# Norm gains multiplied into the weights during their split, and turned features copied two tiles at a time

## The chip, the cores and the metric

The kernel runs on one core of a Trainium2 chip. The metric is the device time of one execution in microseconds (us). A core has a matrix engine (TensorE, here PE, with its weight loads as PEld), a vector engine (VectorE, here DVE), a scalar engine (ScalarE, here ACT), GpSimd (POOL) and a queue engine (SyncE, SP) that issues the DMA transfers. Each engine runs its own instructions in order and waits on semaphores for the others. SBUF is the on-chip memory of 128 partitions, PSUM holds the results of the matrix engine in 8 banks of 512 float32 per partition.

## What is computed

Four transformer layers on 256 tokens of width 1024, in float32. Each begins its two or three parts with a norm that has a gain vector `g` of one number for each of the 1024 features, and the normed tokens go straight into a matrix product:

```
def rms_norm(x, g):
    xf = x.astype(jnp.float32)
    y = xf * lax.rsqrt(jnp.mean(xf * xf, axis=-1, keepdims=True) + EPS)
    return (y * g.astype(jnp.float32)).astype(x.dtype)

for l in range(DEPTH):                       # first block
    h = rms_norm(x, attn_norm_g[l])
    proj = h @ w_in[l]                       # attention branches, pooling, gates
    ...
    x = x + merged @ w_out[l]
    hf = rms_norm(x, ffn_norm_g[l])
    u = depthwise_conv(hf @ ffn_w_up[l], ffn_conv_w[l], ffn_conv_b[l])
    ...
    x = x + (jax.nn.silu(u_gate) * u_val) @ ffn_w_down[l]
```

A second block of two layers follows: a mixer (stick-breaking attention, then dilated attention), a feed-forward part and a gated embedding, each of which starts with such a norm (`g_mix_pre_2`, `g_ffn_pre_2`, `g_ple_2`).

## The kernel before

**Products from halves.** Every float32 operand is held as two fp32r tiles, `high` (the value rounded to fp32r) and `low` (what is left), and each product is the sum of three matrix passes: high by high, high by low, low by high. So both the weights and the features are split, each by one instruction on ACT (high) and one on DVE (low).

**Weights.** They come from HBM in 476 units of at most 1024 columns: a unit is `nk` row tiles (128 rows of the weight matrix, on the partitions) of `w` columns next to each other. With w = 512 or 416 a unit has two row tiles, with w = 256 four. A unit is loaded by SP into one of 4 buffers `w_raw`, copied by ACT into one of 6 buffers `w_high` (L1444, step "split"), and DVE writes `w_raw - w_high` into `w_low` (L1890). ACT may overwrite a `w_high` only when PE is done with the unit six before it. `Plan.prefetch` puts the split of unit n+5 ahead of the matrix work of unit n, so ACT and DVE run five units ahead of PE where nothing else holds them. PE waits for `w_low` of its unit.

**Features.** Where a norm stands, PE turns (transposes) the tokens by 128x128 blocks into a PSUM bank. ACT copies them out as `x_high`, multiplied by the gain of each feature, which lies on the partition then, and DVE writes `bank * gain - x_high` into `x_low`. The norm's `1/rms` per token is applied elsewhere (to the tokens before the turn, or to the product). Two forms exist. Step `turn` (stages 0, 2, 4 and 7; ACT L1452, DVE L1899) handles all 256 tokens of two feature tiles; there are four for a stage. Step `turn_t` (stages 1, 3, 5, 6, 8 and 9; ACT L1463, DVE L1928) handles 128 tokens of two feature tiles; there are eight for a stage, in two groups of four, one group for each half of the tokens. In both forms ACT and DVE issue one instruction for each feature tile, since each has its own gain column. The next turn into a bank waits for the `x_low` of the one before, and so does the first product that reads it.

**Order.** `Plan` writes one list of steps, and every engine goes through it and issues what is its own. Around a norm the list interleaves turns, sums of squares (ACT L1472 and L1481, DVE L1909) and the splits of the coming units. Stages 0, 2, 4, 5 and 8 also need a `row`: DVE writes two diagonal tiles from `1/rms` (L1958, `squares`), and PE multiplies them by ones (L1149). It stands four units into the new part, or after the tokens of stage 5 or 8.

## Time and profile before

| | us |
|---|---|
| median of 3 runs | 1540.28 |
| lowest, highest | 1540.03, 1543.84 |
| the profiled execution | 1539.27 |
| its span from first to last instruction | 1537.5 |
| PE busy | 1493.6 (97%) |
| DVE busy | 1045.8 (68%) |
| ACT busy | 841.4 (55%) |
| DVE on `w_low` (476 splits) | 570.3 |
| ACT on `w_high` (476 splits) | 495.0 |

The granted clock of PE was 0.999 of full over the span. The profile gives for each engine its busy time, for each group of equal instructions their count and mean, and for each idle time of an engine the instruction that ended it. A timeline row has the start, the time from the start of the first to the end of the last instruction of the row, and in brackets the idle time ahead of it and its releaser. Instructions of one engine overlap a little, so the start of the next instruction tells what one costs in a row.

### The profile page before, as it was taken

The numbers are of one execution on the slowest core, as the hardware profiler recorded it, in microseconds if no ns is written. First come the engines' busy times: TensorE is split into PE (matmuls) and PEld (weight loads), VectorE is DVE, ScalarE is ACT, GpSimd is POOL, SyncE is SP. The second block draws the span as 40 slices with busy tenths as digits, with TensorE's granted clock in tenths as the row PEclk, the third lists the DMA queues.
The fourth block names the chain that finished last, engine by engine and source line by source line (L and its number), as shares of the span: only waits on it lengthen the run. The fifth ranks groups of instructions, "written<-read, shape, count | busy, mean of one in ns | idle before, by whom it ended". The sixth has DMA issues, their size and how long they took to land.

```text
span 1537.5 us, 23829 instructions
## 1 busy us (share of the span) xinstructions
PE 1493.6 (97%) x9824; PEld 1340.0 (87%) x9824; DVE 1045.8 (68%) x1545; ACT 841.4 (55%) x1237; POOL 59.1 (4%) x70
## 2 busy tenths in 40 slices
PE   6999999999999999999999999999999998999998
PEld 5998988998899989799989977998888886799886
DVE  5798677786578877687855567665467557766446
ACT  5465556565456565665643476454456446555434
POOL 1110000000021000000000001000010000100001
PEclk9999999999999999999999999999999999999999
DMA  7543355556555435555566533655656550455661
GB/s 243 161 151 119 129 169 167 186 179 205 182 167 173 130 96 165 173 170 195 173 197 212 167 96 110 208 183 192 193 161 224 181 188 29 160 176 179 205 192 69
DMA packets 72572, 255.73 MB, mean 166 GB/s; under 512 B 8336, under 2 KB 9360, under 8 KB 72464
## 3 DMA queue, kind: packets, MB, share of 16 engines
q1 hardware_dynamic: 72176, 253.78, 51.0%
q8 instruction: 77, 1.26, 0.3%
q10 hardware_dynamic: 288, 0.43, 0.1%
q14 instruction: 31, 0.25, 0.1%
HBM read 253.14 MB, written 1.05 MB: 165 GB/s over the span
## 4 chain that ended last, share of the span: by engine, by line
PE 91%; DVE 5%; ACT 2%; issue 1%; POOL 0%; DVEq 0%; ACTq 0%; POOLq 0%
PE psum L1060 14%; PE psum L1063 14%; PE psum L1062 14%; PE psum L1069 13%; PE psum L1073 13%; PE psum L1071 13%; PE psum L1018 3%; DVE w_low L1890 2%; PE psum L1212 1%; PE psum L1297 1%; PE psum L1242 1%; ACT w_high L1444 1%; DVE dil_weights L2337 1%; DVE x_low L1928 0%; PE psum L1371 0%
## 5 line engine op out<-in xcount | busy, mean ns | idle before, releaser
L1890 DVE TENSOR_TENSOR w_low<-w_raw,w_high 128x1024 fp32r<-128x1024 f32 (+1 forms) x476 | 570.3, 1212 | 267.8 <-ACT w_high L1444 266.3
L1444 ACT ACTIVATE w_high<-w_raw 128x1024 fp32r<-128x1024 f32 (+1 forms) x476 | 495.0, 1050 | 334.4 <-PE psum L1073 188.1
L1060 PE MATMUL psum<-x_high,w_high 128*128 128x256 f32 x1504 | 429.9, 286 | 0.0
L1062 PE MATMUL psum<-x_low,w_high 128*128 128x256 f32 x1504 | 425.5, 283 | 0.0
L1063 PE MATMUL psum<-x_high,w_low 128*128 128x256 f32 x1504 | 425.4, 283 | 0.0
L1060 PEld LDWEIGHTS psum<-x_high,w_high 128*128 128x128 f32 x1504 | 288.4, 192 | 5.3 <-issue 4.6
L1062 PEld LDWEIGHTS psum<-x_low,w_high 128*128 128x128 f32 x1504 | 288.5, 192 | 0.3
L1063 PEld LDWEIGHTS psum<-x_high,w_low 128*128 128x128 f32 x1504 | 288.4, 192 | 0.0
L1069 PE MATMUL psum<-w_high,ff_high 128*128 128x512 f32 x256 | 100.0, 391 | 0.0
L1071 PE MATMUL psum<-w_low,ff_high 128*128 128x512 f32 x256 | 99.6, 389 | 0.0
L1073 PE MATMUL psum<-w_high,ff_low 128*128 128x512 f32 x256 | 99.6, 389 | 0.0
L1069 PE MATMUL psum<-w_high,x_high 128*128 128x512 f32 (+2 forms) x208 | 79.5, 382 | 5.7 <-DVE w_low L1890 4.7
L1073 PE MATMUL psum<-w_high,x_low 128*128 128x512 f32 (+2 forms) x208 | 77.3, 372 | 0.0
L1071 PE MATMUL psum<-w_low,x_high 128*128 128x512 f32 (+2 forms) x208 | 77.2, 371 | 0.0
L1069 PE MATMUL psum<-w_high,x_high_next 128*128 128x512 f32 x192 | 75.7, 394 | 0.0
L1071 PE MATMUL psum<-w_low,x_high_next 128*128 128x512 f32 x192 | 74.8, 390 | 0.0
L1073 PE MATMUL psum<-w_high,x_low_next 128*128 128x512 f32 x192 | 74.8, 389 | 0.0
L1069 PE MATMUL psum<-w_high,ffn_high 128*128 128x512 f32 x176 | 68.7, 390 | 0.0
L1071 PE MATMUL psum<-w_low,ffn_high 128*128 128x512 f32 x176 | 68.5, 389 | 0.0
L1073 PE MATMUL psum<-w_high,ffn_low 128*128 128x512 f32 x176 | 68.5, 389 | 0.0
L1060 PE MATMUL psum<-x_high_next,w_high 128*128 128x256 f32 x224 | 63.5, 284 | 0.0
L1063 PE MATMUL psum<-x_high_next,w_low 128*128 128x256 f32 x224 | 63.4, 283 | 0.0
(264 smaller groups left out, 2389.5 us busy)
## 6 DMA issues: line engine op xcount, KB each, us to landing
w_raw<-in_weights SPq DMA_DIRECT2D x462, 512.0 KB, 4.1
w_raw<-in_weights SPq DMA_DIRECT2D x8, 416.0 KB, 5.7
rows<-in_second_rows SPq DMA_DIRECT2D x4, 512.0 KB, 4.8
w_raw<-in_weights SPq DMA_DIRECT2D x6, 256.0 KB, 2.6
residual<-in_x SPq DMA_DIRECT2D x2, 512.0 KB, 5.9
out<-residual SPq DMA_DIRECT2D x2, 512.0 KB, 2.7
dil_masks<-in_consts SPq DMA_DIRECT2D x1, 576.0 KB, 5.6
rows<-in_pool_w SPq DMA_DIRECT2D x2, 256.0 KB, 5.9
```

What stands on the lines that cost most here:

```text
L1018: return eng.transpose(out, src, ident)
L1060: eng.matmul(o, wh[:, j, cut], high[:, k, :], start=k == 0 and f % 2 == 0, stop=False, skip_group_check=True)
L1062: eng.matmul(o, wh[:, j, cut], low[:, k, :], start=False, stop=False, skip_group_check=True)
L1063: d = eng.matmul(o, wl[:, j, cut], high[:, k, :], start=False, stop=end, skip_group_check=True)
L1069: eng.matmul(o, high[:, k, cut], wh[:, j, :], start=k == 0, stop=False, skip_group_check=True)
L1071: eng.matmul(o, high[:, k, cut], wl[:, j, :], start=False, stop=False, skip_group_check=True)
L1073: d = eng.matmul(o, low[:, k, cut], wh[:, j, :], start=False, stop=end, skip_group_check=True)
L1212: d = eng.matmul(bank[4 + i][:, t * SEQ:(t + 1) * SEQ], qt[i][:, t * P:(t + 1) * P], kt[i], start=True, stop=True)
L1242: d = eng.matmul(bank[6][HD * i:HD * i + HD, 0:SEQ], val, m["probt"][i][:, kt * SEQ:(kt + 1) * SEQ], start=kt == 0, stop=kt == TT - 1, ski ...
L1297: d = eng.matmul(o, m, r, start=False, stop=True, skip_group_check=True)
L1444: act(self.unit_view(self.wh, u), raw, ACT.Copy).then_inc(sem("w_high"), 1)
L1890: tt(self.unit_view(self.wl, u), raw, self.unit_view(self.wh, u), ALU.subtract).then_inc(sem("w_low"), 1)
```

## The change

A unit whose rows are the features of a norm now takes the gain in its split: `high = round(w_raw * gain)` and `low = w_raw * gain - high`. The gain is a number for each row, and a row tile has its own gain column, so the split is one instruction for each row tile. Units of other products are split as before. 304 of the 476 units have a norm ahead of them: 284 of 2 x 512 columns, 8 of 2 x 416 and 12 of 4 x 256. The turned features are then copied without a gain, two feature tiles at a time: `turn` and `turn_t` issue one instruction on ACT and one on DVE, 64 steps in all.

```
+    def unit_gain(self, u):
+        g = {"proj": STAGE_MIX, "gates_early": STAGE_MIX, "gates": STAGE_MIX, "ffn_up": STAGE_FFN,
+             "sb_in": (STAGE_SB,), "sb_values": (STAGE_SB,), "dil_in": (STAGE_DIL,), "dil_qk": (STAGE_DIL,),
+             "dil_values": (STAGE_DIL,), "ff_in": STAGE_FF, "ple_gate": STAGE_PLE}.get(u["name"])
+        return None if g is None else self.gain(g[u["layer"]])[:, u["k0"]:u["k0"] + u["nk"]]
 # ACT
-                act(self.unit_view(self.wh, u), raw, ACT.Copy).then_inc(sem("w_high"), 1)
+                gain, high = self.unit_gain(u), self.unit_view(self.wh, u)
+                if gain is None:
+                    act(high, raw, ACT.Copy).then_inc(sem("w_high"), 1)
+                else:
+                    if not (u["name"] in ("proj", "gates_early", "gates", "ffn_up") and u["layer"] == 0):
+                        q.wait_ge(sem("cols_loaded"), 32)
+                    for j in range(u["nk"]):
+                        c = slice(j * u["w"], (j + 1) * u["w"])
+                        d = act(high[:, c], raw[:, c], ACT.Copy, scale=gain[:, j:j + 1])
+                    d.then_inc(sem("w_high"), 1)
 ...
-                for i in range(2):
-                    k = 2 * part + i
-                    d = act(self.features[g][0][:, k, t * P:(t + 1) * P], bank[b][:, i * P:(i + 1) * P], ACT.Copy,
-                            scale=gain[:, k:k + 1])
-                d.then_inc(sem("tokens_high"), 1)
+                act(self.features[g][0][:, 2 * part:2 * part + 2, t * P:(t + 1) * P], got, ACT.Copy
+                    ).then_inc(sem("tokens_high"), 1)
 # DVE
-                tt(self.unit_view(self.wl, u), raw, self.unit_view(self.wh, u), ALU.subtract
-                   ).then_inc(sem("w_low"), 1)
+                gain, high, low = self.unit_gain(u), self.unit_view(self.wh, u), self.unit_view(self.wl, u)
+                if gain is None:
+                    tt(low, raw, high, ALU.subtract).then_inc(sem("w_low"), 1)
+                else:
+                    for j in range(u["nk"]):
+                        c = slice(j * u["w"], (j + 1) * u["w"])
+                        d = stt(low[:, c], raw[:, c], gain[:, j:j + 1], high[:, c], ALU.mult, ALU.subtract)
+                    d.then_inc(sem("w_low"), 1)
 ...
-                for i in range(2):
-                    k = 2 * part + i
-                    d = stt(low[:, k, c], bank[b][:, i * P:(i + 1) * P], gain[:, k:k + 1], high[:, k, c], ALU.mult,
-                            ALU.subtract)
-                d.then_inc(sem("tokens_low"), 1)
+                tt(low, got, high, ALU.subtract).then_inc(sem("tokens_low"), 1)
```

Step `turn` changes in the same way (`x_high` and `x_low` of 512 columns, one instruction each). The program of PE, POOL and SP is the same instruction for instruction. On ACT and DVE the steps stand in the same order, and only the number of instructions in a step changes. Two places matter.

At the first norm DVE writes the `w_low` of three units ahead of the diagonal tiles of `row`; the same stands at stage 2. Before:

```order
L1899 SCALAR_TENSOR_TENSOR x_low<-psum,cols,x_high 128x256 x4
L1909 ISA squares,stat<-residual 128x512
L1909 ISA stat 128x1
L1918 SCALAR_TENSOR_TENSOR stat<-stat 128x2
L1890 TENSOR_TENSOR w_low<-w_raw,w_high 128x1024 x3
L1958 TENSOR_SCALAR squares<-consts,stat 128x128 x2
```

Now:

```order
L1911 TENSOR_TENSOR x_low<-psum,x_high 128x512 x2
L1919 ISA squares,stat<-residual 128x512
L1919 ISA stat 128x1
L1928 SCALAR_TENSOR_TENSOR stat<-stat 128x2
L1904 SCALAR_TENSOR_TENSOR w_low<-w_raw,cols,w_high 128x512 x4
L1904 SCALAR_TENSOR_TENSOR w_low<-w_raw,cols,w_high 128x256 x4
L1963 TENSOR_SCALAR squares<-consts,stat 128x128 x2
```

Three instructions on `w_low` became eight, the last four those of a unit of 256 columns, and four on `x_low` became two.

At stage 1, between the output product and the feed-forward part, DVE writes two units ahead of the first half's `x_low`. Before:

```order
L1938 TENSOR_TENSOR residual<-residual,psum 128x512 x2
L1945 SCALAR_TENSOR_TENSOR stat<-stat 128x1
L1951 TENSOR_SCALAR scratch<-residual,stat 128x512
L1890 TENSOR_TENSOR w_low<-w_raw,w_high 128x1024 x2
L1928 SCALAR_TENSOR_TENSOR x_low<-psum,cols,x_high 128x128 x4
L1890 TENSOR_TENSOR w_low<-w_raw,w_high 128x1024
L1928 SCALAR_TENSOR_TENSOR x_low<-psum,cols,x_high 128x128 x4
L1938 TENSOR_TENSOR residual<-residual,psum 128x512 x2
```

Now:

```order
L1943 TENSOR_TENSOR residual<-residual,psum 128x512 x2
L1950 SCALAR_TENSOR_TENSOR stat<-stat 128x1
L1956 TENSOR_SCALAR scratch<-residual,stat 128x512
L1904 SCALAR_TENSOR_TENSOR w_low<-w_raw,cols,w_high 128x512 x4
L1935 TENSOR_TENSOR x_low<-psum,x_high 128x2x128 x2
L1904 SCALAR_TENSOR_TENSOR w_low<-w_raw,cols,w_high 128x512 x2
L1935 TENSOR_TENSOR x_low<-psum,x_high 128x2x128 x2
L1943 TENSOR_TENSOR residual<-residual,psum 128x512 x2
```

Each `w_low` became two instructions, and each four of `x_low` two.

## Rows read from the trace of the kernel before

**Rows 1.** The page, busy time of each engine (share of the span, instructions).

```profile
PE 1493.6 (97%) x9824; PEld 1340.0 (87%) x9824; DVE 1045.8 (68%) x1545; ACT 841.4 (55%) x1237; POOL 59.1 (4%) x70
```

**Rows 2.** Waits of PE: for whom, us in total, times, longest.

```profile
PE psum L1149 <- DVE squares L1958: 4.4, 4, 1.6
PE psum L1018 <- DVE x_low L1928: 4.2, 5, 1.2
```

**Rows 3.** Groups by shape: busy us, mean ns of one, idle before them.

```profile
L1890 DVE TENSOR_TENSOR w_low<-w_raw,w_high 128x1024 fp32r<-128x1024 f32 x462 | 558.3, 1222 | 261.4 <-ACT w_high L1444 259.8
L2262 DVE SCALAR_TENSOR_TENSOR residual<-scratch,stat,residual 128x512 f32<-128x512 f32 x16 | 11.3, 749 | 0.9
L1851 DVE SCALAR_TENSOR_TENSOR sb_out_low<-psum,sb_out_high 128x256 fp32r<-128x256 f32 x8 | 3.4, 424 | 13.8 <-ACT sb_out_high L1429 13.8
...
L1444 ACT ACTIVATE w_high<-w_raw 128x1024 fp32r<-128x1024 f32 x462 | 484.3, 1058 | 314.6 <-PE psum L1073 180.9 <-PE psum L1063 121.2 <-DMA w_raw<-in_weights 11.7
L1487 ACT ACTIVATE scratch<-residual,stat 128x512 f32<-128x512 f32 x4 | 2.9, 724 | 3.5 <-POOL stat L2445 3.5
```

**Rows 4.** Timeline of DVE in stage 5: start, us, instruction.

```profile
951.86 1.41 DVE L2262 SCALAR_TENSOR_TENSOR residual<-scratch,stat,residual 128x512 f32<-128x512 f32 x2
953.19 1.22 DVE L1890 TENSOR_TENSOR w_low<-w_raw,w_high 128x1024 fp32r<-128x1024 f32 x1
```

**Rows 5.** Timeline of ACT, DVE and PE at stage 2, up to its row.

```profile
424.69 1.66 DVE L1899 SCALAR_TENSOR_TENSOR x_low<-psum,cols,x_high 128x256 fp32r<-128x256 f32 x4 [1.13 <-ACT x_high L1452]
...
428.84 1.06 ACT L1444 ACTIVATE w_high<-w_raw 128x1024 fp32r<-128x1024 f32 x1 [0.94 <-PE psum L1073]
...
429.93 1.23 DVE L1890 TENSOR_TENSOR w_low<-w_raw,w_high 128x1024 fp32r<-128x1024 f32 x1 [0.44 <-ACT w_high L1444]
431.07 0.47 DVE L1958 TENSOR_SCALAR squares<-consts,stat 128x128 f32<-128x128 f32 x2
...
431.60 0.71 PE L1149 MATMUL psum<-squares,consts 128*128 128x128 f32 x4 [0.62 <-DVE squares L1958]
```

**Rows 6.** Timeline of ACT, DVE and PE at stage 0, the first norm.

```profile
9.90 1.57 ACT L1452 ACTIVATE x_high<-psum,cols 128x256 fp32r<-128x256 f32 x4
...
24.16 3.50 DVE L1890 TENSOR_TENSOR w_low<-w_raw,w_high 128x1024 fp32r<-128x1024 f32 x3
...
28.11 0.71 PE L1149 MATMUL psum<-squares,consts 128*128 128x128 f32 x4 [0.62 <-DVE squares L1958]
```

**Rows 7.** Timeline of DVE and PE at the row of stage 4.

```profile
836.44 0.48 DVE L1958 TENSOR_SCALAR squares<-consts,stat 128x128 f32<-128x128 f32 x2
836.97 0.71 PE L1149 MATMUL psum<-squares,consts 128*128 128x128 f32 x4
```

**Rows 8.** Timeline of ACT, DVE and PE at stage 1, both halves of the tokens.

```profile
224.66 1.99 ACT L1444 ACTIVATE w_high<-w_raw 128x1024 fp32r<-128x1024 f32 x2
...
225.74 2.36 DVE L1890 TENSOR_TENSOR w_low<-w_raw,w_high 128x1024 fp32r<-128x1024 f32 x2 [1.22 <-ACT w_high L1444]
...
228.01 1.12 DVE L1928 SCALAR_TENSOR_TENSOR x_low<-psum,cols,x_high 128x128 fp32r<-128x128 f32 x4
...
228.76 0.86 PE L1018 MATMUL psum<-consts,scratch 128*128 128x128 f32 x4 [1.17 <-DVE x_low L1928]
...
237.94 0.86 PE L1018 MATMUL psum<-consts,scratch 128*128 128x128 f32 x4 [0.76 <-DVE x_low L1928]
```

**Rows 9.** Timeline of ACT and PE at stage 5, up to its row.

```profile
958.00 1.99 ACT L1444 ACTIVATE w_high<-w_raw 128x1024 fp32r<-128x1024 f32 x2
...
963.02 0.71 PE L1149 MATMUL psum<-squares,consts 128*128 128x128 f32 x4 [1.59 <-DVE squares L1958]
```

**Rows 10.** Timeline of DVE and PE in the attention part of layer 0.

```profile
95.22 0.61 DVE L2109 TENSOR_SCALAR head_work<-head_work,stat 128x256 f32<-128x256 f32 x2
...
99.17 1.04 PE L1018 MATMUL psum<-consts,head_work 128*128 128x128 f32 x8
...
105.81 0.43 DVE L1851 SCALAR_TENSOR_TENSOR mixed_low<-psum,mixed_high 128x256 fp32r<-128x256 f32 x1 [1.05 <-ACT mixed_high L1429]
```

More of the change, by code:

```diff
@@ L1448, in scalar @@
                 q.wait_ge(sem("features_turned"), at(*step))
-                b, gain = TURN_BANKS[j], self.gain(g)
-                for i in range(2):
-                    k = 2 * j + i
-                    d = act(self.features[g][0][:, k, :], bank[b][:, i * SEQ:(i + 1) * SEQ], ACT.Copy,
-                            scale=gain[:, k:k + 1])
-                d.then_inc(sem("features_high"), 1)
+                act(self.features[g][0][:, 2 * j:2 * j + 2, :], by_tile(bank[TURN_BANKS[j]]), ACT.Copy
+                    ).then_inc(sem("features_high"), 1)
             elif kind == "turn_t":
                 g, t, part = key
-                b, gain = token_bank(g, part), self.gain(g)
+                got = bank[token_bank(g, part)][:, 0:2 * P].rearrange("p (k s) -> p k s", k=2)
                 q.wait_ge(sem("tokens_turned"), at(*step))
-                q.wait_ge(sem("cols_loaded"), 32)
-                for i in range(2):
-                    k = 2 * part + i
-                    d = act(self.features[g][0][:, k, t * P:(t + 1) * P], bank[b][:, i * P:(i + 1) * P], ACT.Copy,
-                            scale=gain[:, k:k + 1])
-                d.then_inc(sem("tokens_high"), 1)
+                act(self.features[g][0][:, 2 * part:2 * part + 2, t * P:(t + 1) * P], got, ACT.Copy
+                    ).then_inc(sem("tokens_high"), 1)
             elif kind == "square_t":
@@ L1895, in vector @@
                 q.wait_ge(sem("features_high"), at(*step))
-                b, gain = TURN_BANKS[j], self.gain(g)
-                for i in range(2):
-                    k = 2 * j + i
-                    d = stt(self.features[g][1][:, k, :], bank[b][:, i * SEQ:(i + 1) * SEQ], gain[:, k:k + 1],
-                            self.features[g][0][:, k, :], ALU.mult, ALU.subtract)
-                d.then_inc(sem("features_low"), 1)
+                high, low = (a[:, 2 * j:2 * j + 2, :] for a in self.features[g])
+                tt(low, by_tile(bank[TURN_BANKS[j]]), high, ALU.subtract).then_inc(sem("features_low"), 1)
             elif kind == "square":
@@ L1921, in vector @@
                 g, t, part = key
-                b, gain = token_bank(g, part), self.gain(g)
-                high, low = self.features[g]
-                c = slice(t * P, (t + 1) * P)
+                got = bank[token_bank(g, part)][:, 0:2 * P].rearrange("p (k s) -> p k s", k=2)
+                high, low = (a[:, 2 * part:2 * part + 2, t * P:(t + 1) * P] for a in self.features[g])
                 q.wait_ge(sem("tokens_high"), at(*step))
-                for i in range(2):
-                    k = 2 * part + i
-                    d = stt(low[:, k, c], bank[b][:, i * P:(i + 1) * P], gain[:, k:k + 1], high[:, k, c], ALU.mult,
-                            ALU.subtract)
-                d.then_inc(sem("tokens_low"), 1)
+                tt(low, got, high, ALU.subtract).then_inc(sem("tokens_low"), 1)
             elif kind == "residual_t":
```

## The prediction

> **What bounds the kernel now.** I read the page's busy times first. PE is busy 1493.6 of 1537.5 us, DVE 68% and ACT 55% [rows 1]. So the matrix passes set the time, and the change leaves every one of them in place. What ACT and DVE do costs time only where PE stands still for them, and PE stands still for 44 us in all. The second view is the waits of PE, read as a list of places: which instruction of PE waited, for whom, how long. Two kinds of wait hang on what the change touches. PE waits 4.4 us for the diagonal tiles of the `row` and 4.2 us for `x_low` of the half-token turns [rows 2]. The rest of the waits (first loads, attention heads, dilated attention, the last gate) have no split with a gain and no turn directly ahead of them. The third view is the timeline around each place: what stood in the queue of ACT and DVE between the last thing they waited for and the thing that PE waited for. Everything there counts one for one, everything else is hidden.
>
> Away from the norms the work has a cushion. The groups by shape show ACT idle 314.6 us ahead of its splits, almost all of it waiting for PE to give a slot back, and DVE idle 261.4 us waiting for ACT [rows 3]. The splits run five units ahead.
>
> **The price of a split.** Before, ACT takes 1.06 us for a unit and DVE 1.22 us [rows 3]. Afterwards each takes two instructions with a gain column. No row shows exactly that form, so I take the nearest. On DVE, L2262 is a multiply by a column and a second operand over 512 columns in SBUF, 0.749 us alone [rows 3]. Two of them in a row are followed after 953.19 - 951.86 = 1.33 us by the next instruction [rows 4], where a whole `w_low` is followed after 431.07 - 429.93 = 1.14 us [rows 5]. So DVE pays **+0.19 us a unit**. On ACT, L1487 is a copy of 512 columns with a column scale, 0.724 us [rows 3]; two without overlap would be 1.45. Two splits in a row take 1.99 where two means give 2.12 [rows 8, 3], so neighbours overlap by about 0.1, and a pair ends after 1.35 us: **+0.29 us a unit**. For a unit of four tiles of 256, DVE's four take 1.66 - 0.08 = 1.58 us to the next start [rows 5] against 1.14, **+0.43**, and ACT's four take 1.57 us [rows 6] against 1.06, **+0.51**.
> The bounds are wide. Below, both could cost nothing, if the pieces overlapped completely. Above, with no overlap, the pairs cost 2 x 0.749 - 1.222 = +0.28 and 2 x 0.724 - 1.058 = +0.39, and the four-tile unit about +0.65 and +0.8. I take the middle values, since they are read from instructions in a row, as the splits are.
> Over 304 units that is some 60 us more on DVE and 95 on ACT, of which nearly all lies beside PE's work.
>
> **The price of a turn.** Four half-token pieces of `x_low` take 1.12 us [rows 8]. Two pieces of 256 from PSUM without a gain take 0.424 each [rows 3], about 0.77 with the same overlap: **-0.35** for a group of four. What PE waits for first is one pair, before 0.26 + 0.34 = 0.60, now 0.42: **-0.18**.
>
> **Stage 2, the row.** The third split starts when PE frees its slot, at 428.84. ACT ends, DVE writes `w_low` at 429.93, the diagonals at 431.07, and PE goes on at 431.60 after 0.62 of waiting [rows 5]. The turns lie ahead of 428.84, so their saving is swallowed by the wait for the slot. The unit is one of 256 columns, as the order of the changed program shows, so the chain grows by 0.51 + 0.43 = **+0.94**.
>
> **Stage 0.** Here DVE runs its three units without a gap, 24.16 to 27.58, and the diagonals and the 0.62 wait follow [rows 6]. Two ordinary units and one of four tiles: 2 x 0.19 + 0.43 = **+0.81**. The shorter turns ahead of it save about as much as the two splits between them add.
>
> **Stage 4.** No wait is printed, but PE starts 0.53 after the diagonals as it does at stage 2 [rows 7, 5], so the chain is just touching PE. An ordinary unit, started by PE's slot: 0.29 + 0.19 = **+0.48**.
>
> **Stages 1 and 3** are alike. The first `w_low` starts when the first `w_high` is there (+0.29), two follow in a row (+0.38), then `x_low` [rows 8]. The first pair is late by 0.67 - 0.18 = 0.49, and so is PE at 228.76. But that is not kept: PE idles again at the second half of the tokens, and what reaches it there along DVE is 0.67 - 0.35 + 0.19 - 0.35 = +0.16. The second half adds one split and one pair, 0.29 + 0.19 - 0.18 = 0.30, which PE meets at 237.94, where it waits 0.76 already [rows 8]. So **+0.46** each, 0.92 for both.
>
> **Stages 5 and 8** are alike. Here the turns gain first. Two groups of four precede the splits on both engines, and nothing from outside holds them in between but PE, which gains too, so ACT reaches its first split (958.00) 0.7 earlier. Then +0.29 and three `w_low` at +0.19 follow before the diagonals that PE waits 1.59 for [rows 9]: -0.70 + 0.29 + 0.57 = +0.16, **+0.32** for both.
>
> **Stages 6, 7 and 9** have no row. PE is not printed as waiting for their turns, and I count nothing.
>
> **The sum.** 0.94 + 0.81 + 0.48 + 0.92 + 0.32 = **+3.5 us**. The profiled execution took 1539.27 us, 1.8 more than its span, so it would become 1542.8. It lies 1.0 below the median of the runs, and the forecast for the median is 1540.28 + 3.5 = **1543.8 us**, 0.23% slower.
>
> One rule of the Trainium skill would make it less. The rows make a DVE unit with a gain 0.19 us dearer. The Trainium skill (Vector Engine (DVE) Microarchitecture Reference, section 5.2, Measured stream behaviour on trn2) puts the fixed part of an instruction in a row at about 75 ns and does not tell a gain column from a constant, so a cut in two would cost 0.075 and one in four 0.225. By that the same sum is an estimate of about +2.0 and the time 1542.3. I keep the rows, since the pair of L2262 shows 1.33 us directly.
>
> **Rivals.** (A) *DVE becomes the bound in the attention parts*, and the kernel is plainly slower. While the gates are multiplied, three splits with gains fall into each pair of heads, and DVE has next to no gap: from 89 to 105.8 it waits once, for 1.05 us [rows 10], and five units stand there, which ask for 0.95, or for 1.4 at the upper price. Against it: the softmax is done at 95.83 and PE turns it only at 99.17 [rows 10], so a backlog must reach 3.3 us to be felt. If it did, 3 x 0.19 for each of 4 pairs in 2 layers is 4.6 us more: 1548.4.
> (B) *The pieces cost nothing on the path* and only the shorter turns count. Then stages 1 and 3 gain 0.35 + 0.35 + 0.18 = 0.9 each, 5 and 8 about 0.4 each (the slot of the third split holds them then), stage 0 about 0.2, together 2.8: 1537.5. For it speaks that ACT and DVE have half of their time free; against it, the third view: at these places they run instruction after instruction.
> (C) *Nothing moves*, because gains and losses cancel or the pieces lie under PE after all: 1540.3. The edit then doesn't do what it says for the path: it shifts work from where PE waits to where it doesn't, and back.
>
> **Chances.** Forecast 0.63 (own range 1541.5 to 1547), A 0.13, B 0.14, C 0.10. A measurement can tell about 0.3%, that is 4.6 us: faster is below 1535.7, slower above 1544.9. The forecast lies 1.1 from that bound. With the upper prices the same places give about 6.5 us, 1546.8, so I put 0.20 of its 0.63 beyond. Slower: 0.20 + 0.13 = 0.33. Faster: the far part of B, 0.05. Same: 0.43 + 0.09 + 0.10 = 0.62. The range is 1539.0 to 1548.0: it leaves out most of B and the end of A.
>
> **What would show it.** In the profile of the changed kernel DVE's splits of 512 should have a mean near 0.75 us and ACT's near 0.72, DVE's busy time should rise by 50 to 80 us and ACT's by 70 to 110, and PE's should stay within 2. PE's wait for the diagonals should grow from 4.4 to about 7 us in total, with those of stages 0 and 2 near 1.4 to 1.6 and one of about 0.5 at stage 4. A wait of PE for `head_work` or for `w_low` in the attention parts would speak for A. Waits for `x_low` that shrink at stages 1 and 3 would speak for B. The prediction is wrong if the pieces are much cheaper or dearer than L2262 and L1487, or if a place that I called hidden has less room than the rows show.

## The result and the profile of the changed kernel

The changed kernel takes **1547.86 us** (median of 5 executions, 1546.12 to 1548.52), against 1540.28 before: a ratio of 1.0042, 95% interval 1.0028 to 1.0055. Run again as e12_after_again it gave 1547.8 against 1542.62, 1.0037 (1.0023 to 1.0051). It is slower, by less than half a per cent. The forecast had the sign and named half of the size: +3.5 us where +7.6 came out by these medians.

The page's busy times, the waits of PE (for whom, us in total, times, longest) and the groups by shape of the changed kernel, which answer to [rows 1 to 3]:

```profile
PE 1495.4 (97%) x9824; PEld 1343.2 (87%) x9824; DVE 1092.9 (71%) x1809; ACT 911.2 (59%) x1501; POOL 49.5 (3%) x70
```

```profile
PE psum L1156 <- DVE squares L1963: 8.2, 5, 2.1
...
PE psum L1025 <- DVE x_low L1935: 5.9, 6, 1.6
...
PE psum L1076 <- DVE x_low L1911: 1.4, 1, 1.4
PE psum L1025 <- DVE mla_heads L2083: 1.2, 1, 1.2
```

```profile
L1904 DVE SCALAR_TENSOR_TENSOR w_low<-w_raw,cols,w_high 128x512 fp32r<-128x512 f32 x568 | 395.0, 747 | 120.2 <-ACT w_high L1459 119.6
...
L1459 ACT ACTIVATE w_high<-w_raw,cols 128x512 fp32r<-128x512 f32 x568 | 373.9, 717 | 119.0 <-PE psum L1070 60.6 <-PE psum L1080 46.6 <-DMA w_raw<-in_weights 11.6
```

PE has the same 9824 instructions and 1.8 us more of work. DVE is 47 us busier and ACT 70. The prices of one piece were foreseen: 747 ns for 749, 717 for 724. The wait for the diagonals has grown from 4.4 to 8.2 us, where about 7 was written. The last of the four waits is new: PE waits 1.2 us for `mla_heads`, in the attention of layer 1. The forecast's sum had nothing there.

**Where the 8.6 us went.** Both programs give PE the same instructions in the same order, so the start of each can be compared between two traces. The profiled executions differ by 8.6 us of span. For each place, the table gives by how much more (or less) time PE needed to get through it than in the profile of before; the columns to the right belong to experiments further down. Stretches in which TensorE's clock fell later than stage 0 are left out of it. The third column is the control: it is the kernel before, executed again (e0), against its own first profile.

| place | forecast | e0, before again | changed | e12, the same again | e1: pairs only | e3: and cut | e4: and ACT's scale |
| --- | --- | --- | --- | --- | --- | --- | --- |
| up to the row of stage 0 | +0.81 | +1.43 | +1.30 | +2.17 | -0.73 | +0.03 | +1.24 |
| attention, layer 0 | 0 | +0.02 | +0.46 | +0.45 | 0 | +0.13 | +0.32 |
| stage 1 | +0.46 | 0 | +0.19 | +0.22 | -1.13 | -0.66 | -0.47 |
| stage 2, the row | +0.94 | +0.01 | +1.10 | +1.10 | 0 | +0.48 | +0.65 |
| attention, layer 1 | 0 | +0.03 | +1.70 | +1.68 | 0 | +0.09 | +0.52 |
| stage 3 | +0.46 | -0.02 | +0.17 | +0.17 | -1.14 | -0.68 | -0.50 |
| stage 4, the row | +0.48 | 0 | +0.54 | +1.38 | 0 | +0.16 | +0.27 |
| stage 5 | +0.16 | -0.02 | -0.05 | -0.06 | -1.08 | -0.93 | -0.79 |
| stages 6 and 7 | 0 | 0 | -0.26 | -0.23 | -0.65 | -0.50 | -0.51 |
| stage 8 | +0.16 | 0 | 0, and clock | 0 | -1.33 | -0.92 | -0.79 |
| stage 9 | 0 | 0 | -0.27 | -0.31 | -0.64 | -0.50 | -0.53 |
| sum | +3.5 | +1.4 | **+4.9** | +6.6 | **-6.7** | **-3.3** | **-0.6** |

The control says how far to trust a row. Past stage 0 the unchanged kernel repeats itself within 0.03 us, but up to the row of stage 0 it differs from itself by 1.4 us. So what this table gives the change at stage 0 (+1.30, +2.17) is not its price, and the sums carry this spread: +4.9 and +6.6 against the first profile of before, 3.5 and 5.2 against e0. The rows past stage 0 add to +3.6 (4.4 in e12, where the weights for stage 4 came late: ACT waited 2.92 us for one of them there). Of the 8.6 us that the two spans differ by, another 0.5 is the first load (the constants), which came later, and 3.2 us are TensorE's clock: 1.7 in the dilated attention and 1.5 at stage 8.

**The clock.** Here are stretches of 5 us of the changed kernel; after the busy times of the five engines come PEclk, the granted clock as a share of 2.4 GHz, the DMA share and GB/s.

```profile
1275.00:1280.00 5.00, 3.24 (x24) 2.16 (x24) 1.13 (x5) 2.99 (x6) 0.00 (x0) 0.83 0.26 97
1280.00:1285.00 5.00, 3.19 (x20) 2.63 (x20) 4.20 (x14) 2.40 (x5) 0.00 (x0) 0.50 0.00 0
...
1340.00:1345.00 5.00, 5.00 (x33) 5.00 (x32) 1.42 (x2) 2.60 (x4) 0.00 (x0) 0.69 0.81 287
```

At 0.50 the engine runs at 1.2 GHz. The profile of before has 1.00 in all three places. It would be easy to call this an effect of the change; the first experiment shows that such a fall also comes without it.

### The profile page after: what moved, and what is told of

Same layout as the page of the kernel before. It is cut to its first block, busy times and chain, and to the rows that moved or that the text cites. A ratio compares the mean times of both kernels' runs of the same rounds, so it can differ in the third digit from the quotient of the medians.

```text
span 1546.1 us, 24356 instructions
## 1 busy us (share of the span) xinstructions
PE 1495.4 (97%) x9824; PEld 1343.2 (87%) x9824; DVE 1092.9 (71%) x1809; ACT 911.2 (59%) x1501; POOL 49.5 (3%) x70
## 4 chain that ended last, share of the span: by engine, by line
PE 86%; DVE 7%; ACT 3%; issue 1%; DMA 1%; POOL 0%; SPq 0%; ACTq 0%; DVEq 0%
PE psum L1067 13%; PE psum L1070 13%; PE psum L1069 13%; PE psum L1076 13%; PE psum L1080 13%; PE psum L1078 13%; PE psum L1025 3%; DVE w_low L1904 3%; ACT w_high L1459 1%; PE psum L1219 1%; PE psum L1304 1%; PE psum L1249 1%; PE psum L1342 1%; DVE dil_weights L2342 1%; DMA w_raw<-in_weights 1%
## 5 line engine op out<-in xcount | busy, mean ns | idle before, releaser
L1904 DVE SCALAR_TENSOR_TENSOR w_low<-w_raw,cols,w_high 128x512 fp32r<-128x512 f32 (+2 forms) x632 | 424.2, 724 | 132.1 <-ACT w_high L1459 131.5
L1459 ACT ACTIVATE w_high<-w_raw,cols 128x512 fp32r<-128x512 f32 (+2 forms) x632 | 402.8, 699 | 128.3 <-PE psum L1070 62.0
L1900 DVE TENSOR_TENSOR w_low<-w_raw,w_high 128x1024 fp32r<-128x1024 f32 (+1 forms) x172 | 206.0, 1205 | 128.5 <-ACT w_high L1453 128.5
L1453 ACT ACTIVATE w_high<-w_raw 128x1024 fp32r<-128x1024 f32 (+1 forms) x172 | 178.0, 1041 | 164.4 <-PE psum L1080 121.3
```

Of the source, the lines that this page charges most:

```text
L1453: act(high, raw, ACT.Copy).then_inc(sem("w_high"), 1)
L1459: d = act(high[:, c], raw[:, c], ACT.Copy, scale=gain[:, j:j + 1])
L1900: tt(low, raw, high, ALU.subtract).then_inc(sem("w_low"), 1)
L1904: d = stt(low[:, c], raw[:, c], gain[:, j:j + 1], high[:, c], ALU.mult, ALU.subtract)
```

## Experiments

### e0: the kernel before, once more

No edit. 

> The kernel before, unchanged, for the granted clock of its executions. The changed kernel's profile shows the clock at 1.2 GHz in two stretches, near 1279 to 1286 us and 1340 to 1344 us, worth about 1.7 and 1.5 us there; the profile of before has neither. Theory 1 (the falls belong to the changed kernel): all executions of before have a mean clock of 0.999 and a time within 1 us of 1540.3. Theory 2 (the falls can happen in either kernel, and the two executions of before at 1542.9 and 1543.8 us are such): some execution of before shows 0.996 to 0.998 and 1.5 to 4 us more than the others.

Measured: 1541.93 us median over 12 executions (1540.32 to 1544.93). The profiled one had a mean clock of 0.995 and a span of 1543.0, and its stretches show the same fall at the same place:

```profile
1275.00:1280.00 5.00, 3.06 (x22) 2.18 (x18) 2.83 (x8) 1.95 (x4) 0.00 (x0) 0.50 0.00 0
1280.00:1285.00 5.00, 5.00 (x28) 3.45 (x28) 3.02 (x10) 1.79 (x5) 0.00 (x0) 0.52 0.00 0
```

The same twelve matrix instructions, of the profile of before first, then of this execution (timeline: start, us, instruction, what was waited for):

```profile
1271.98 1.57 PE L1335 MATMUL psum<-dil_k,dil_q 64*128 64x256 f32 x12 [1.14 <-DVE stat L2337]
```

```profile
1274.15 2.62 PE L1335 MATMUL psum<-dil_k,dil_q 64*128 64x256 f32 x12 [1.14 <-DVE stat L2337]
```

Same program, same wait of 1.14 us ahead, 1.57 us once and 2.62 the other time. Theory 2 holds.

Stage 0 differs too. Its rows, in the first profile of before and then in this one:

```profile
19.49 1.06 ACT L1444 ACTIVATE w_high<-w_raw 128x1024 fp32r<-128x1024 f32 x1 [0.71 <-DMA w_raw<-in_weights]
...
22.74 0.42 PE L1069 MATMUL psum<-w_high,x_high 128*128 128x416 f32 x1 [0.93 <-DVE x_low L1899]
```

```profile
20.72 1.06 ACT L1444 ACTIVATE w_high<-w_raw 128x1024 fp32r<-128x1024 f32 x1 [1.50 <-DMA w_raw<-in_weights]
...
23.97 0.43 PE L1069 MATMUL psum<-w_high,x_high 128*128 128x416 f32 x1 [1.86 <-DVE x_low L1899]
```

And two microseconds of this one's stretches, in the form shown above:

```profile
26.00:28.00 2.00, 2.00 (x8) 1.91 (x7) 1.74 (x2) 0.50 (x1) 1.17 (x1) 0.50 0.39 84
```

A load came later, PE waited 0.93 us longer, and behind that wait the granted clock was 0.50. Together this is the control's 1.4 us.

In the comparisons of the experiments the kernel before was executed 76 times (12 as e0, 64 beside the other kernels):

| mean granted clock | before, times | before, median us | changed, times | changed, median us | difference |
|---|---|---|---|---|---|
| 0.999 | 13 | 1540.5 | 0 | | |
| 0.998 | 27 | 1541.8 | 3 | 1546.7 | +4.8 |
| 0.997 | 9 | 1542.3 | 2 | 1547.8 | +5.4 |
| 0.996 | 16 | 1543.8 | 4 | 1548.0 | +4.2 |
| 0.995 | 11 | 1543.4 | 1 | 1549.4 | +6.0 |

Their median is 1542.0, so the 1540.28 that the forecast was added to, a median of three executions, lies 1.7 us low. At equal clocks the change costs 4.2 to 5.4 us, the single execution at 0.995 aside, and the forecast's +3.5 has to be held against this number. The table's 3.6 past stage 0 leaves 0.6 to 1.8 of it for stage 0.

### e1 and e2: the two halves of the change

e1: whole splits, and the norms' scale vectors left out everywhere; the paired copies stay.

```diff
-        return None if g is None else self.gain(g[u["layer"]])[:, u["k0"]:u["k0"] + u["nk"]]
+        return None
```

> Splits whole as before, turned features copied two tiles at a time; the norms' scale vectors are left out everywhere, so no instruction has a scale column there. The forecast's price of the paired copies: four half-token pieces at -0.35 us, the first pairs of stages 0, 2, 4, 5, 8 at -0.18 us each, so about 1538 us, 2 to 3 us under before. If instead the paired copies bring nothing on the path (the row steps and transfers end last), 1540.3 within 1 us. If the clock falls come with the paired copies, over 1541 us with a mean granted clock of 0.996 to 0.998.

Measured: **1533.85 us** (0.9954 of before, 0.9941 to 0.9967), where about 1538 was expected. That is 6.7 us less at equal clock, by the table and by the executions (1533.6 and 1533.9 at 0.999, against 1540.5). The forecast's price of the copies, -2.8 in its rival B, was less than half of it. Stage 1 shows part of what was left out (the changed kernel first, then e1):

```profile
231.47 0.68 PE L1025 MATMUL psum<-consts,scratch 128*128 128x128 f32 x4 [1.64 <-DVE x_low L1935]
...
237.46 0.66 PE L1025 MATMUL psum<-consts,scratch 128*128 128x128 f32 x4 [1.20 <-ACT scratch L1495]
...
240.56 0.68 PE L1025 MATMUL psum<-consts,scratch 128*128 128x128 f32 x4 [1.05 <-DVE x_low L1935]
```

```profile
228.47 0.68 PE L1025 MATMUL psum<-consts,scratch 128*128 128x128 f32 x4 [0.98 <-DVE x_low L1935]
...
234.26 0.66 PE L1025 MATMUL psum<-consts,scratch 128*128 128x128 f32 x4 [0.98 <-ACT scratch L1495]
236.90 0.68 PE L1025 MATMUL psum<-consts,scratch 128*128 128x128 f32 x4 [0.60 <-DVE x_low L1935]
```

The turn of four tiles that takes 0.68 us here took 0.86 in [rows 8], twice a stage: its third tile started 0.43 us after the first where it starts 0.25 after it in e1, since it had to wait for the second `x_low` pair. The list of waits doesn't print so short a gap. The middle wait was 1.36 us before:

```profile
235.12 0.66 PE L1018 MATMUL psum<-consts,scratch 128*128 128x128 f32 x4 [1.36 <-ACT scratch L1487]
```

It is booked on ACT, but its chain starts on DVE. In the profile of before DVE's second group of `x_low` runs into the residual, and the squares, the statistics on GpSimd and the `scratch` copy follow one behind the other:

```profile
230.18 1.12 DVE L1928 SCALAR_TENSOR_TENSOR x_low<-psum,cols,x_high 128x128 fp32r<-128x128 f32 x4
231.22 1.27 DVE L1938 TENSOR_TENSOR residual<-residual,psum 128x512 f32<-128x512 f32 x2
231.93 0.63 ACT L1472 ACTIVATE squares<-residual 128x512 f32<-128x512 f32 x1 [1.58 <-DVE residual L1938]
```

So PE reaches the second half when DVE is through both groups of `x_low`, and in e1 it gets there 0.76 us earlier, where the forecast had 0.35 + 0.35. The second pair takes another 0.19 off (0.18 foreseen). What the forecast lacked is the last 0.18, which is PE's own second turn: together -1.13 against the -0.9 of rival B.

e2: the changed kernel, with the copies made one tile at a time, still without a scale.

```diff
-                tt(low, got, high, ALU.subtract).then_inc(sem("tokens_low"), 1)
+                for i in range(2):
+                    d = tt(low[:, i, :], got[:, i, :], high[:, i, :], ALU.subtract)
+                d.then_inc(sem("tokens_low"), 1)
```

(and alike in the three other copies). 

> The changed kernel with its turned features copied one tile at a time, without a scale column: the split part of the change alone. Theory 1 (the paired copies save what the forecast says): 2 to 3 us over the changed kernel, about 1550 us. Rival (a copy without a scale column is as cheap in two instructions as in one): within 1 us of the changed kernel's 1547.9.

Measured: 1550.17 us, 2.3 over the changed kernel (2.0 and 2.1 at the clocks 0.997 and 0.995), as theory 1 expected; stages 1 and 3 cost +0.56 each instead of +0.19. So the pairing is worth 2.0 to 2.3 us beside these splits. The other 4 to 5 us of e1's gain are put down to the scale column that the copies no longer have. That is a difference and not shown by a run: no kernel here has whole splits and single copies without a scale.

### e3 and e4: what in the splits costs

e3: the splits in 128-row pieces, but plain.

```diff
-                        d = act(high[:, c], raw[:, c], ACT.Copy, scale=gain[:, j:j + 1])
+                        d = act(high[:, c], raw[:, c], ACT.Copy)
...
-                        d = stt(low[:, c], raw[:, c], gain[:, j:j + 1], high[:, c], ALU.mult, ALU.subtract)
+                        d = tt(low[:, c], raw[:, c], high[:, c], ALU.subtract)
```

> The changed kernel, its splits cut into 128-row pieces as there, but as a plain copy (ScalarE) and a plain subtraction (VectorE); the norms' scale vectors are left out everywhere. e1_pairs_only took 1533.9 us with whole splits, the changed kernel 1547.9 us. Theory 1 (a cut alone costs its fixed part, the scale column the rest; VectorE's piece falls from 747 to some 640 ns as its whole tile of twice the size takes 1222, ScalarE's from 717 to some 630): about half of the 14 us, 1540 us, within 2. Rival (the cut is all of it, whatever the operand): within 1.5 us of 1547.9.

Measured: **1537.86 us**, 4.0 over e1 and 10.0 under the changed kernel; at equal clocks 2.7 to 3.3 over the one and 8.7 to 9.4 under the other. It lies just below theory 1's 1538 to 1542. Its groups by shape:

```profile
L1904 DVE TENSOR_TENSOR w_low<-w_raw,w_high 128x512 fp32r<-128x512 f32 x568 | 361.8, 686 | 124.4 <-ACT w_high L1459 123.8
...
L1459 ACT ACTIVATE w_high<-w_raw 128x512 fp32r<-128x512 f32 x568 | 324.0, 625 | 144.6 <-PE psum L1070 77.1 <-PE psum L1080 55.5 <-DMA w_raw<-in_weights 11.7
```

The multiply by a scale column costs 747 - 686 = 61 ns an instruction on DVE and 717 - 625 = 92 ns on ACT. (Whether a constant scale would cost the same wasn't run.) The cut is the smaller part. The chain of stage 2 shows both, as each kernel walks it: ACT's split, DVE's split, then the diagonals. First e1, then e3, then the changed kernel:

```profile
427.61 1.06 ACT L1453 ACTIVATE w_high<-w_raw 128x1024 fp32r<-128x1024 f32 x1 [1.21 <-PE psum L1080]
...
428.70 1.23 DVE L1900 TENSOR_TENSOR w_low<-w_raw,w_high 128x1024 fp32r<-128x1024 f32 x1 [1.05 <-ACT w_high L1453]
```

```profile
428.94 1.34 ACT L1459 ACTIVATE w_high<-w_raw 128x256 fp32r<-128x256 f32 x4 [1.12 <-PE psum L1080]
...
430.31 1.43 DVE L1904 TENSOR_TENSOR w_low<-w_raw,w_high 128x256 fp32r<-128x256 f32 x4 [1.13 <-ACT w_high L1459]
```

```profile
431.26 1.71 ACT L1459 ACTIVATE w_high<-w_raw,cols 128x256 fp32r<-128x256 f32 x4 [0.87 <-PE psum L1080]
433.00 1.67 DVE L1904 SCALAR_TENSOR_TENSOR w_low<-w_raw,cols,w_high 128x256 fp32r<-128x256 f32 x4 [1.07 <-ACT w_high L1459]
...
435.12 0.71 PE L1156 MATMUL psum<-squares,consts 128*128 128x128 f32 x4 [1.72 <-DVE squares L1963]
```

1.06 + 1.23 = 2.29, 1.34 + 1.43 = 2.77, 1.71 + 1.67 = 3.38: the differences, +0.48 and +1.09, are the table's numbers for this place. That e1 has 0 there says that no turn reaches it, as the forecast had it.

For two DVE splits in a row at stage 1, four pieces take 2.50 us in e3 against 2.36 whole in e1, so the cut alone is 0.07 us a unit. That agrees with the 75 ns which the Trainium skill names (Vector Engine (DVE) Microarchitecture Reference, section 5.2, Measured stream behaviour on trn2). With the scale column the same four take 2.74: another 0.06 an instruction, which that section does not tell. With the cut alone the chain of stage 2 lengthens by e3's 0.48, with the column by 1.10.

e4: ACT's splits as in the changed kernel, DVE's whole.

```diff
-                if gain is None:
+                if True:
                     tt(low, raw, high, ALU.subtract).then_inc(sem("w_low"), 1)
```

> The changed kernel with ScalarE's splits in pieces as there and VectorE's whole as before; the low parts of the weights lack the scale. Theory 1 (VectorE is the engine that ends the row steps, the transfers of features and the turn of q in attention): the split part costs only ScalarE's terms, 3 us or less over the 1533.9 us of e1_pairs_only, so 1534 to 1538 us. Rival (ScalarE's pieces hold up VectorE, which follows it unit by unit): over 1542 us.

Measured: 1540.01 us, between the two theories. By the executions at equal clocks ACT's pieces bring about 5 us over e1 and DVE's another 6.3 to 7.9; the table has 6.1 and 5.5, but with the spread of stage 0 in it. At stage 2, 0.65 of the 1.10 us is ACT's. Both engines are on the path wherever one works behind the other on the same unit, so neither alone is "the" cause.

### e7: the gates' splits whole

```diff
-        g = {"proj": STAGE_MIX, "gates_early": STAGE_MIX, "gates": STAGE_MIX, "ffn_up": STAGE_FFN,
+        g = {"proj": STAGE_MIX, "gates_early": STAGE_MIX, "ffn_up": STAGE_FFN,
```

> The changed kernel with the gate weights' units (those that VectorE and ScalarE split during attention) whole as before; the gates lack the norm's scale. The changed kernel's attention parts are longer by 0.45 and 1.7 us than those of before. Theory 1 (rival A in a weaker form: VectorE, without a gap in layer 1 from 498 to 528 us, reaches the copy of k late and TensorE's turn of q waits 1.2 us for it): the wait goes, 2 us come off, 1546 us. Rival (the loss comes from elsewhere in attention): within 0.7 us of 1547.9.

Measured: 1546.96 us by the median, 0.9 less (1.0 at the clock 0.996). By the same comparison of PE's starts the attention of layer 1 went from +1.70 to **0.00** and that of layer 0 from +0.46 to +0.07, 2.1 us together. The whole time fell by only half of that. In the profiled execution stage 0 took 0.6 us more than in the changed kernel's profile, which is within what it varies by; the low clock took 1.7 us more in the dilated attention and 1.5 less at stage 8. Layer 1 in three kernels: before, changed, e7.

```profile
522.04 0.42 DVE L1851 SCALAR_TENSOR_TENSOR mixed_low<-psum,mixed_high 128x256 fp32r<-128x256 f32 x1 [0.35 <-ACT mixed_high L1429]
522.38 0.74 DVE L2078 TENSOR_SCALAR mla_heads<-psum,cols 96x512 f32<-96x512 f32 x1
...
524.09 0.60 PE L1018 MATMUL psum<-consts,mla_tokens 128*96 128x128 f32 x4
```

```profile
528.06 0.42 DVE L1859 SCALAR_TENSOR_TENSOR mixed_low<-psum,mixed_high 128x256 fp32r<-128x256 f32 x1 [0.16 <-ACT mixed_high L1436]
528.41 0.74 DVE L2083 TENSOR_SCALAR mla_heads<-psum,cols 96x512 f32<-96x512 f32 x1
...
529.29 0.61 PE L1025 MATMUL psum<-consts,mla_tokens 128*96 128x128 f32 x4 [1.23 <-DVE mla_heads L2083]
```

```profile
526.25 0.74 DVE L2083 TENSOR_SCALAR mla_heads<-psum,cols 96x512 f32<-96x512 f32 x1
...
527.98 0.60 PE L1025 MATMUL psum<-consts,mla_tokens 128*96 128x128 f32 x4
```

`mla_heads` is DVE's copy of the turned k, which frees the PSUM bank for the turn of q. Before, it ended at 523.12 and PE came at 524.09: a slack of 0.97 us. In the changed kernel DVE had stood still for only 0.16 us twice since 498.6 (0.35 twice over the same work before), its copy ended at 529.15, and PE stood still for 1.23 us. With whole splits the slack is 527.98 - 526.99 = 0.99 again. Not all of the loss is DVE's: e4, with DVE's splits whole, keeps 0.32 and 0.52 us in the two attention parts, which are then ACT's.

### e5 and e6: the diagonals one unit earlier

The changed kernel (e5) and the kernel before (e6), with DVE's two instructions for the diagonals in a step of their own, one weight unit ahead of the `row`:

```diff
+        self.after(3, lambda: add("diag", g))
         self.after(4, lambda: add("row", g))
...
-            elif kind == "row":
+            elif kind == "diag":
                 g = key[0]
                 q.wait_ge(sem("r_ready"), at("rstd", g))
```

(DVE's branch only; in stages 5 and 8 it stands after the second unit of the pass.) 

> The changed kernel, with VectorE's writing of the diagonals (two instructions of the row step) taken out of the row step's place and put one weight unit earlier in VectorE's order, in stages 0, 2, 4, 5 and 8; SyncE, ScalarE and TensorE keep their order. Theory 1 (TensorE's wait for the diagonals is the two split instructions that VectorE has queued ahead of them): the five waits, 8.2 us together, fall under 2 us, and the time falls by 4 to 7 us to 1541 to 1544 us. Rival (the sums of the norm arrive late, and the order behind them does not matter): waits stay over 6 us, time within 1.5 us of 1547.9. Should the clock fall no more near 1279 and 1340 us because the kernel reaches those places with other waits ahead, up to 3 us more come off.

> The kernel before with VectorE's two instructions for the diagonals one weight unit earlier, as in e5_after_early_diag; nothing of the change is in it. The waits for the diagonals there are 0.62, 0.62, 0 and 1.6 twice, with the unit's work of VectorE ahead of them 1.2 us. Theory 1 (a queue order that costs before too): five row steps shorter by 0.7, 0.7, 0.2, 1.7 and 1.7 us, about 5 us under the 1541.8 us of before: 1536 to 1538 us. Rival (the wait only moves to the transfers behind the row step, which VectorE then reaches later): within 1.5 us of before.

Measured: e5 **1540.16 us**, 6.2 to 6.7 less than the changed kernel at equal clock (1541.5 for 1548.0 at 0.996, 1540.0 for 1546.7 at 0.998), a little below theory 1's 1541 to 1544. All five waits for the diagonals are gone from the list. e6 took 1539.27 us, 0.9981 of before (0.9971 to 0.999), 3.0 less by the medians and 2.5 to 2.9 at the clocks 0.998 and 0.999, where 5 was expected. The rest came back at stages 5 and 8. In stage 5 of e6:

```profile
961.77 0.48 DVE L1961 TENSOR_SCALAR squares<-consts,stat 128x128 f32<-128x128 f32 x2 [0.60 <-POOL stat L2452]
...
962.17 2.35 DVE L1893 TENSOR_TENSOR w_low<-w_raw,w_high 128x1024 fp32r<-128x1024 f32 x2
962.31 0.71 PE L1152 MATMUL psum<-squares,consts 128*128 128x128 f32 x4
...
964.44 1.40 DVE L2274 TENSOR_SCALAR scratch<-psum,stat 128x512 f32<-128x512 f32 x2
...
966.98 1.09 PE L1021 MATMUL psum<-consts,scratch 128*128 128x128 f32 x8 [1.09 <-ACT scratch L1710]
```

PE reaches its row without a wait, but the two splits that used to stand ahead of the diagonals now stand behind them, ahead of the two scalings that the next turn needs, and PE waits 1.09 us there. Of the 1.6 us that e6 gains at the row, 1.25 is given back, in both stages, and as much in e5: the rival of e6 is right for these two places and wrong for stages 0, 2 and 4, where nothing comes back.

At clock 0.998 the change costs 1540.0 - 1539.3 = 0.7 us with early diagonals and 4.8 without. So 4 of its 4.8 us hung on one thing in DVE's order: splits queued ahead of a small step for which PE waits.

### e9: the change only where it gains

Scales in the weights and paired copies after stage 4, features scaled as before up to stage 4, diagonals early everywhere.

```diff
-        g = {"proj": STAGE_MIX, "gates_early": STAGE_MIX, "gates": STAGE_MIX, "ffn_up": STAGE_FFN,
-             "sb_in": (STAGE_SB,), "sb_values": (STAGE_SB,), "dil_in": (STAGE_DIL,), "dil_qk": (STAGE_DIL,),
+        g = { "dil_in": (STAGE_DIL,), "dil_qk": (STAGE_DIL,),
...
+                if g <= STAGE_SB:
+                    ...
```

> The change made only in the stages after stage 4 (scale in the weights of ff_in, ple_gate and the dilated attention, copies in pairs there), stages 0 to 4 with the scale in the feature copies as before, and VectorE's diagonals one unit earlier everywhere, as in e6_before_early_diag. Theory 1 (the change costs in stages 0, 2 and 4 and in the two attention parts, and gains 0.3 us each in stages 6, 7 and 9; with the diagonals early stages 5 and 8 gain 0.7 us each too): 1 to 2.5 us under the 1539.3 us of e6_before_early_diag, 1537 to 1538.3 us, so some 4 us under before. Rival (the clock falls and the transfers behind the row step take it back): 1539.3 within 0.8 us, or over it.

Measured: **1537.33 us**, 0.9956 of before (0.9943 to 0.997), 1.9 under e6, as theory 1 expected. The ratio flatters it, since most executions of before beside it had a low mean clock: at 0.998 and 0.999 it is 4.2 and 4.5 us under before. By the starts of PE, stages 5 and 8 each take 0.98 us less than before (e6: 0.28), and stages 6, 7 and 9 the 0.26 and 0.31 that the changed kernel gains there too. It is the fastest of the kernels here that compute everything.

### e10 and e11: the scale on GpSimd

GpSimd multiplies the scale into the raw tile in place; the splits are whole and plain.

```diff
+            if kind == "split":
...
+                    for j in range(u["nk"]):
+                        c = slice(j * u["w"], (j + 1) * u["w"])
+                        d = ts(raw[:, c], raw[:, c], gain[:, j:j + 1], None, ALU.mult)
+                    d.then_inc(sem("w_scaled"), 1)
```

> The changed kernel with the norms' scale vectors multiplied into the raw weights by GpSimd (busy 49.5 us of 1546 in the changed kernel), in place and in 128-row pieces ahead of the splits; ScalarE and VectorE split whole units by a plain copy and subtraction, as before, and the turned features are copied in pairs. Theory 1 (the price is the cut and the scale column on the two busy engines): up to the 1533.9 us of e1_pairs_only, 1534 to 1537 us. Rival (GpSimd's piece, of a kind and size that no trace here shows, takes longer than the 1.3 us that a unit's pitch of 2.9 us leaves for two of them, or holds up VectorE; its steps for the norms queue behind it): the splits come late, over 1545 us, up to some hundreds of us more.

> e10_pool_scales with VectorE's diagonals one unit earlier. Theory 1: 2 to 3 us under e10_pool_scales, as e6_before_early_diag under before, 1531 to 1535 us. Rival (GpSimd's power for the norm now queues behind its scaling, so the sums come late and the early place makes VectorE wait ahead of its splits): not under e10_pool_scales, or over it by 1 us or more.

Measured: 1873.35 and 1870.93 us, a fifth slower. Groups by shape and waits of PE in e10:

```profile
L2438 POOL TENSOR_SCALAR w_raw<-w_raw,cols 128x512 f32<-128x512 f32 x568 | 1055.0, 1877 | 281.9 <-DMA w_raw<-in_weights 281.8
```

```profile
PE psum L1071 <- DVE w_low L1896: 57.2, 40, 6.5
PE psum L1160 <- DVE squares L1955: 49.4, 5, 11.5
```

A piece takes GpSimd 1877 ns where DVE's takes 747. Two of them are 3.75 us, more than PE's mean share of a unit (1495 us / 476 = 3.1), so GpSimd becomes the bound wherever a scale is needed, and its steps for the norms queue behind: the waits for the diagonals are 49 us. The rival is right. The early diagonals brought 2.4 us here too, theory 1's 2 to 3 less (its 1531 to 1535 us are far off), with the waits for them at 26.4 us.

### e12: the changed kernel once more

No edit. 

> The changed kernel, unchanged, beside before on the same chip, for the granted clock of its executions. In the runs here before had a mean clock of 0.999 in about one execution of four (1540.4 us), 0.998 in two of four (1541.8 us), and 0.995 to 0.997 in the rest (1542 to 1545 us). Theory 1 (the clock falls at stage 8 come with the longer wait for the diagonals, so the changed kernel has them nearly always): no execution at 0.999, and a median of 1547 to 1548.5 us, 4.5 to 6 us over before's. Theory 2 (the falls are as frequent as in before, and the five executions had bad luck): a quarter at 0.999, near 1545 us, and a median of 1546 to 1547 us.

Measured: 1547.8 us (1546.65 to 1549.37), 5.2 over the median of before beside it, and no execution at 0.999: the numbers that theory 1 named. But its profile has no fall at stage 8 although the wait for the diagonals is there, so the wait does not always bring the fall. Of ten executions of the changed kernel none was at 0.999, of 76 of before 13 were: at that rate ten in a row without one happen about one time in seven. Whether the change makes the falls more frequent is open. Stage 4 cost 1.38 instead of 0.54 and the start 2.17 instead of 1.30 in this execution, with the same program.

## Why the prediction was right, and where its sum was short

**Right: the bound and the sign.** PE's work stayed within 2 us. The busy times rose by 47 us on DVE, just under the 50 to 80 foreseen, and by 70 on ACT (70 to 110).

**Right: the prices of a split.** In the chain of stage 2 ACT's four-tile unit grew by 0.65 (0.51 foreseen, from copies out of PSUM) and DVE's by 0.44 (0.43). The 0.19 us for two pieces on DVE is what four pieces against two whole units show, (2.74 - 2.36) / 2. One side sum was off: with 0.075 for a cut in two and 0.225 for one in four, the forecast's own terms are 0.74 + 0.38 + 0.37 + 0 - 0.37 = +1.1 and not about +2.0. The forecast itself didn't use it.

**Right: stage 2, stage 4 and the inner steps of stage 1.** +1.10 for +0.94 and +0.54 for +0.48. At stage 1 PE's first `x_low` came 0.47 us later (0.49 foreseen), PE reached the second half 0.10 later (0.16), and that half's wait brought +0.28 (0.30).

**Mis-sized: the price of a turn.** The step "what PE waits for first is one pair: -0.18" took the wait ahead of PE's turn and not the turn itself. The runs showed that PE's own turn of four shrinks too, from 0.86 to 0.68 us, since its third tile no longer waits for the second pair. That counts wherever PE doesn't stand still again behind it: in the second half of stages 1 and 3, and in the stages without a row, where nothing had been counted. Stages 1 and 3 cost 0.36 together instead of 0.92, and stages 5 to 9 nothing or less than nothing (-0.6 for the +0.3 foreseen). Left to itself this error would have made the forecast 1.5 us too high.

**Wrong path: stage 0.** The forecast let DVE run its three units without a gap, and had ACT out of it: +0.81. In the changed kernel the third split waits for PE's slot and DVE waits for ACT, as at stage 2:

```profile
26.02 1.71 ACT L1459 ACTIVATE w_high<-w_raw,cols 128x256 fp32r<-128x256 f32 x4 [0.76 <-PE psum L1080]
...
27.77 1.67 DVE L1904 SCALAR_TENSOR_TENSOR w_low<-w_raw,cols,w_high 128x256 fp32r<-128x256 f32 x4 [0.36 <-ACT w_high L1459]
```

PE's wait for the diagonals there is 1.70 us in both profiles of the changed kernel, 0.62 in the first profile of before and in e1: +1.08, the chain of stage 2. How much of it lasts in the total is not known within a microsecond, since this stage differs by 1.4 us between two executions of before and by 0.9 between two of the changed kernel.

**Failed: the attention parts.** Rival A was priced from the wrong neighbour. It said that "a backlog must reach 3.3 us to be felt", the slack of the softmax. The tighter release stands one step on: the copy of the turned k, with 0.97 us. Five units at +0.19 already ask for 0.95 of it, and the change brought 1.23 us of waiting on top. e7 shows it by taking the gates' pieces away. So rival A was right as a mechanism at half of its price (2.2 us instead of 4.6), on top of the forecast and not in its place. Neither of the waits that were to speak for it, for `head_work` or `w_low`, came; the wait was for another of DVE's steps.

**Outside the sum: the reference and the clock.** 1.7 us of the 7.6 is that the median of three executions lay low against 76. The one of the three at 1543.84 was a sign of that; I read it as a range and should have moved the middle. The clock and chance have the rest: the ten executions of the changed kernel and the 76 of before have medians 5.9 us apart, and those of e12 5.2.

Against the 4.2 to 5.4 us at equal clocks the forecast was 0.7 to 1.9 short. By the places of the first pair of profiles it lacked attention +2.2, stage 0 +0.5 (the uncertain one) and stage 2 +0.2, and had the turns too dear by 1.5. So it was near in part because two errors had opposite signs. There was luck in the range too: 1547.86 lies 0.14 us inside its upper end of 1548.0, past the forecast's own 1541.5 to 1547, nearer to the 1548.4 of rival A than to 1543.8, and past the 1544.9 from which on the chances counted it as slower, with 0.33 against 0.62 for the same.

## What to carry to other kernels

Price a moved multiply by its operand column as well as by the number of pieces, on every engine that handles the same tile one after the other. Before an engine gets more work in a stretch where it has no gaps, list all things that it releases there and take the smallest slack, not the most visible one. And look first at what is queued ahead of a small step for which the bounding engine waits: moving two short instructions by one place was worth more (6.2 to 6.7 us in the changed kernel) than the whole change cost. Before splitting a difference of a few microseconds into places, compare the unchanged kernel with itself: here one stage moved by 1.4 us on its own.

## What the runs showed of the hardware

- The granted clock of TensorE falls to half for a few us at places with waits, in some executions of a program and not in others with the same waits: 1.57 or 2.62 us for the same twelve matrix instructions. The 76 executions of before had mean clocks from 0.995 to 0.999, and the medians of these groups span 3.3 us.
- A multiply by a per-partition scale column costs 61 ns an instruction on VectorE and 92 ns on ScalarE at 512 columns (e3 against the changed kernel).
- GpSimd takes 1877 ns for a multiply of 128x512 by a column, 1084 ns for 128x256: by these two an estimate of 3.1 ns a column and about 290 ns fixed. VectorE's whole splits had a mean of 1265 ns in that kernel and 1222 in the kernel before.
